# Attention of a hybrid encoder in 56 steps of four score tiles

## The chip, the cores and the metric

The kernel runs on one core of a Trainium2 chip. The metric is the time of one execution on the device in microseconds (us); lower is better. Everything is fp32 data; large products are made in three passes of split operands, and the attention's products are plain fp32, which the chip runs as two records each.

## The reference

Two layers, sequence 1024, width 1024. Each layer: RMS norm, one projection to q, k and v of three head groups, attention in each, output norm per group, output projection with residual, then a SwiGLU FFN. This part is what the change touches:

```python
oa = neighbourhood_attention(rms_norm(q), rms_norm(k), v, rpb)       # A: 4 heads, 2-D window, bias table
ob, _ = banded_attention(q, k, v, 128, slopes[:6], 1, sink)          # B: 6 query heads on 2 key heads
for window, d in ((128, 1), (512, 4), (2048, 16)):                   # C: 6 heads, three dilations
    o, lse = banded_attention(to_sub(q), to_sub(k), to_sub(v), window // (2 * d), slopes[6:], d)
oc = sum(softmax(lse) * o)                                           # merged by the denominators
y = concat([rms_norm(oa, ga), rms_norm(ob, gb), rms_norm(oc, gc)]) @ w_out
# in each: p = exp(sc - max(sc)); o = p @ v / sum(p)
```

## The kernel before, in words

Each engine has its own program, written out by hand, and they meet at semaphores. A layer runs: turned input and value projections, 14 q/k units (`qk_unit_steps`), the attention, the output projection (`out_product`), then the FFN by sums of seven block products. Only the attention changes; its ends reach into the last q/k unit and into the first output products.

The attention is a list of 224 **tiles** per layer. A tile is one head of 128 queries against a window of keys: `n_tiles` gives 24 for each of two bodies of kind c3 (dilation 16, 128 keys wide), 24 for each of two of kind c2 (dilation 4, 192 keys) and 16 for each of the eight query blocks b0, mid (six) and b7: six tiles of group B, six of C's own branch, four of A, 192 to 384 keys wide. Tiles of the dilated bodies come in 16 groups of six (one per head).

What happens to a tile:
- `score` or `score_pair` (L2125, L2133, TensorE): queries x keys into a bank. In the dilated bodies `QS` holds each head's queries padded with zero rows to 128, and a tile is one full-array product; in the blocks two heads lie on the two row halves and are issued as a pair.
- `tmin` (L1418, VectorE): table minus score, with the minimum as running accumulator; writes `T`.
- `exponential` (L1033, ScalarE): exp over `T`.
- `unit` (L2144, TensorE): transposes of `T` in chunks of 128, one unit per tile, into bank 4 or 5; `copy_unit` brings it to `PT`, even units on VectorE, odd ones on ScalarE.
- `weigh` (L2160, TensorE): `PT` x values into bank 6 or 7, in two column halves; `store_result` (L1026, ScalarE) takes each head group to `G4` or `GB`.

`pe_body` (L2185) sets TensorE's order: a dilated body takes one tile per turn, a block two: scores two ahead, transposes of the current, value products two behind. `dve_body` (L1622) follows it tile by tile and puts the finishing of a block (`own_finish`, `late_finish`: sink, merging of branches, squares, scaling of `Y`) between the tiles, one or two small operations per tile. `Y`'s parts are turned by further units (`Y_AT`) and copied to `QK`.

Beside that, GpSimd's `stage` (L1926) gathers the dilated queries of the upper half and the keys for each group (VectorE's `stage_low` the lower half), takes a power of 16 columns (`ROOTS`, L1967), and from block to block merges the branches (`merge`) and takes powers. VectorE makes A's bias tables (`bias_table`) and the last key unit's scaling (`scale_last`). SyncE's queue does, for each of the 16 dilated groups: `store_group` (L783), `spread_roots` in four of them, `load_values` for the group four later, and four loads of bias rows (L747) in the first eight.

## Time and profile before

| | |
|---|---|
| median of 3 runs | 2537.73 us (2536.75 to 2538.58) |
| the profiled execution's own time | 2537.85 us |
| its span, first to last instruction | 2536.1 us |
| TensorE busy | 2448.9 us |
| VectorE busy | 1682.6 us |
| ScalarE busy | 1061.8 us |
| GpSimd busy | 596.7 us |

Busy times are sums of records; a TensorE record is longer than the time it holds the array, as the next one starts inside it. Where TensorE's time goes is therefore read from starts: the distance from the first record of one group to the first of the next.

### The profile page before, as it was taken

The page shows a single profiled execution, that of the slowest core. Times are in us where ns is not written, and L with a number is a line of the kernel's source. Part 1 is how long each engine was busy: PE and PEld are TensorE (multiplying, and loading weights), DVE is VectorE, ACT ScalarE, POOL GpSimd, SP SyncE. Part 2 cuts the span into 40 slices and gives each one's busy share as a digit, 9 for nine tenths or more (in the row PEclk, how much of TensorE's full clock was granted, in tenths as well). Part 3 has the DMA queues.
Part 4 walks back from the last instruction along what each step waited for, and adds up shares of the span by engine and source line. Part 5 has one row for each costly group of instructions (what it writes and reads, how often), then busy time and mean ns, then how long its engine had stood idle before and what let it go on. Part 6 is the DMA issues. An engine that isn't in the chain of part 4 may idle for free. (4 is left out here: it accounts for less than half of the span.)

```text
span 2536.1 us, 39881 instructions
## 1 busy us (share of the span) xinstructions
PE 2448.9 (97%) x14416; PEld 1967.3 (78%) x14416; DVE 1682.6 (66%) x3163; ACT 1061.8 (42%) x2080; POOL 596.7 (24%) x503
## 2 busy tenths in 40 slices
PE   7999999999899999999989999999999999999998
PEld 7887666678688888888788876665777888888887
DVE  5388668864655555689844985688556555556897
ACT  4343656645322222344343336566453222223432
POOL 1000312310554454200010003123015445442000
PEclk9999999999999999999989999999999999999999
DMA  6111520033222221632351216100322222126222
GB/s 239 52 41 42 137 66 21 21 119 104 67 83 78 89 67 52 234 118 68 104 176 51 50 33 149 54 21 21 135 88 75 75 92 84 58 67 253 92 83 96
DMA packets 233420, 225.44 MB, mean 89 GB/s; under 512 B 49668, under 2 KB 191492, under 8 KB 233224
## 3 DMA queue, kind: packets, MB, share of 16 engines
q1 hardware_dynamic: 233224, 222.92, 27.9%
q8 instruction: 112, 1.84, 0.3%
q14 instruction: 84, 0.69, 0.1%
HBM read 171.03 MB, written 51.84 MB: 88 GB/s over the span
## 5 line engine op out<-in xcount | busy, mean ns | idle before, releaser
L2310 PE MATMUL psum<-OPH_t,WH 128*128 128x512 f32 x704 | 276.3, 393 | 17.3 <-DVE WL L1716 7.5
L2310 PE MATMUL psum<-OPL_t,WH 128*128 128x512 f32 x704 | 275.4, 391 | 0.0
L2310 PE MATMUL psum<-OPH_t,WL 128*128 128x512 f32 x704 | 275.3, 391 | 0.0
L1716 DVE TENSOR_TENSOR WL<-RAW,WH 128x512 fp32r<-128x512 f32 x132 | 161.5, 1224 | 161.3 <-ACT WH L1175 161.3
L2343 PE MATMUL psum<-ABH 128*128 128x512 f32 x616 | 240.1, 390 | 1.1 <-DVE X L1802 1.1
L2344 PE MATMUL psum<-ABL,ABH 128*128 128x512 f32 x616 | 239.7, 389 | 0.0
L2345 PE MATMUL psum<-ABH,ABL 128*128 128x512 f32 x616 | 239.7, 389 | 0.0
L1038 ACT ACTIVATE T<-T,G 128x192 f32<-128x192 f32 (+3 forms) x352 | 166.0, 472 | 124.8 <-DVE G L1441 121.0
L2008 POOL TENSOR_TENSOR WS<-RAW 128x512 f32<-128x512 f32 x88 | 157.5, 1789 | 211.4 <-PE psum L2040 169.5
L2310 PE MATMUL psum<-OPH_b,WH 128*128 128x512 f32 x528 | 205.6, 389 | 0.0
L2310 PE MATMUL psum<-OPH_b,WL 128*128 128x512 f32 x528 | 205.4, 389 | 0.0
L2310 PE MATMUL psum<-OPL_b,WH 128*128 128x512 f32 x528 | 205.4, 389 | 0.0
L1716 DVE TENSOR_TENSOR WL<-WS,WH 128x512 fp32r<-128x512 f32 x176 | 144.6, 821 | 83.0 <-ACT WH L1175 82.7
L2157 PE MATMUL psum<-ident,T 128*128 128x128 f32 x920 | 177.9, 286 | 16.5 <-ACT T L1038 10.7
L2038 PE MATMUL psum<-HH,UH 128*128 128x512 f32 x448 | 175.4, 392 | 5.9 <-DVE QK L1381 4.6
L2157 PEld LDWEIGHTS psum<-ident,T 128*128 128x128 f32 x920 | 105.6, 141 | 93.6 <-ACT T L1038 59.1
L2039 PE MATMUL psum<-HL,UH 128*128 128x512 f32 x448 | 175.1, 391 | 0.0
L2040 PE MATMUL psum<-HH,UL 128*128 128x512 f32 x448 | 174.9, 390 | 0.0
L1378 DVE RECIPROCAL RM<-RM 128x512 f32<-128x512 f32 x52 | 174.0, 3346 | 0.0
L2310 PEld LDWEIGHTS psum<-OPH_t,WH 128*128 128x128 f32 x704 | 133.0, 189 | 50.2 <-DVE OPL_t L1722 8.1
L1597 DVE COPY PT<-psum 128x256 f32<-128x256 f32 (+2 forms) x224 | 96.3, 430 | 104.7 <-PE psum L2157 103.9
L2310 PEld LDWEIGHTS psum<-OPH_t,WL 128*128 128x128 f32 x704 | 133.0, 189 | 27.9
(230 smaller groups left out, 5387.5 us busy)
## 6 DMA issues: line engine op xcount, KB each, us to landing
RAW<-in_w_gu SPq DMA_DIRECT2D x176, 256.0 KB, 3.8
WDS<-in_w_down SPq DMA_DIRECT2D x88, 256.0 KB, 2.7
UR<-in_w_in SPq DMA_DIRECT2D x56, 256.0 KB, 3.2
g_mid<-GRES SPq DMA_DIRECT2D x28, 512.0 KB, 2.6
WDK<-in_w_down SPq DMA_DIRECT2D x44, 256.0 KB, 5.3
x_res<-X SPq DMA_DIRECT2D x2, 4096.0 KB, 13.8
PR<-in_w_out SPq DMA_DIRECT2D x32, 256.0 KB, 4.5
X<-x_res SPq DMA_DIRECT2D x2, 4096.0 KB, 13.7
```

Source lines behind the costliest of these rows:

```text
L1038: a.activation(T[:, s % 4, off:off + w], T[:, s % 4, off:off + w], ACT.Exp, scale=-1.0, bias=G[:, 6 * V1 + place_:6 * V1 + place_ + 1]).th ...
L1378: v.reciprocal(RM[:, hf, :], RM[:, hf, :]).then_inc(rec_s, 1)
L1716: v.tensor_tensor(WL[SLOT[i, j]][:, :, :], w_source(i, j), WH[SLOT[i, j]][:, :, :].bitcast(F32), ALU.subtract).then_inc(w_lo, 1)
L2008: g.tensor_tensor(WS[i][:, :, :], first, second, op).then_inc(w_sum, 1)
L2038: t.matmul(dst, sh, mh, start=start, stop=False)
L2039: t.matmul(dst, sh, ml, start=False, stop=False)
L2040: return t.matmul(dst, sl, mh, start=False, stop=stop)
L2157: last = t.transpose(dst[0:src.shape[-1], P * i:P * i + P], src, ident[:, :])
L2310: last = t.matmul(dst[:, :], w[SLOT[i, j]][:, k, :], h[o][:, k, :], start=(i in (1, 5, 6) and k == 0 and part == 0), stop=(i in (2, 3, 4) ...
L2343: t.matmul(dst, ah, bh, start=open_, stop=False, skip_group_check=True)
L2344: t.matmul(dst, ah, bl, start=False, stop=False, skip_group_check=True)
L2345: last = t.matmul(dst, al, bh, start=False, stop=shut, skip_group_check=True)
```

## The change

The attention becomes 56 steps of four tiles, in the same order of tiles. TensorE's step k: scores of tiles 4k to 4k+3 as two pairs on row halves (now also the dilated ones: `QS` holds two heads per 128 rows, and there is no padding), the value products of step k-2's tiles, then the transposes of step k-1's tiles. Transposes are packed: up to four chunks of 128, of one or several tiles, in one bank, with one copy for each pack; the second pack of a step is copied by VectorE (in a step with one pack, that one), all others and all `Y` units by ScalarE. Banks 0, 2, 6, 7, 1, 3 rotate between scores and transposes; the value products have 4 and 5. `T` has eight slots of 384.

The (192-key) tiles of c2 now always have two chunks of 128 against a value tile whose lower rows are zeroed once; their value loads are two DMAs instead of one. `stage_low` is gone: GpSimd gathers both halves. GpSimd also takes over `bias_table`, `scale_last` (the raw unit is first kept by ScalarE's `keep_raw`) and the scaling of `Y`. VectorE's finishing of a block is regrouped into `finish(k, j)`: five places in the first step of the next block, two in its second, five in its third, none in its fourth.

```diff
-        T = sb("T", [P, 4, 640], F32, "W", 0)
-        QS = sb("QS", [P, 12, P], F32, "Q")
+        T = sb("T", [P, 8, 384], F32, "W", 0)
+        QS = sb("QS", [P, 2, 3, P], F32, "Q", 2048)
...
+            TRIO = ((0, 2), (6, 7), (1, 3))
...
+            for k in range(1, GROUPS + 1):
+                rows = steps[k]
+                for n in range(4 * k - 4, 4 * k):
+                    need = len(chunks_of(*tiles[n]))
+                    if not rows or len(rows[-1]["items"]) + need > 4:
+                        pair_ = TRIO[(k + 2) % 3] if len(rows) < 2 else TRIO[k % 3]
+                        rows.append(dict(y=None, items=[], engine=None, bank=pair_[len(rows) % 2], slot=n_pt % 4))
+                        n_pt += 1
...
+                for fam, after in (("b", 6), ("a", 7), ("c", 7)):
...
+                for i, u in enumerate(pt_rows):
+                    u["engine"] = (0 if len(pt_rows) == 1 or i == 1 else 1)
...
+            HIGH_AT = {46: 0, 49: 1, 52: 2, 54: 3}
+            PIECE_AT = {first_group(b) + 1: 13 + b for b in range(3, 7)}
...
-                return bank[2 * (s % 2) if dilated(bd) else s % 4][:, 0:width(bd, s)[0]]
+                return bank[TRIO[(n // 4 + n % 4 // 2) % 3][n % 2]][:, 0:width(*tiles[n])[0]]
...
-                        sp.dma_start(VR[:, slot, :, :], v4[(gi - 8) // 2]).then_inc(vr_in[slot], 16)
+                        sp.dma_start(VR[:, slot, 0, :], v4[j0:j0 + P]).then_inc(vr_in[slot], 16)
+                        sp.dma_start(VR[0:64, slot, 1, :], v4[j0 + P:j0 + P + 64]).then_inc(vr_in[slot], 16)
...
+                def finish(k, j):
+
+                    b, r = divmod(k - first_group(0), 4)
+                    if 0 <= b < MT and r == 2:
+                        if j == 0:
+                            own_min(b)
+                        elif j == 1:
+                            own_shift(b)
+                    b -= 1
...
+                    if r == 0:
+                        if j < 4:
+                            own_sum(b, j)
+                            if j < 2:
+                                branch_min(b, j)
+                            elif j == 2:
+                                branch_shift(b)
                         else:
...
+                            own_heads(b)
...
+                    if r == 1:
+                        if j == 0:
+                            squares(1, YB, 384, b)
+                        elif j == 1:
+                            mean(1, 384)
+                    elif r == 2:
+                        if j == 0:
+                            grid_root(b)
+                        elif j == 1:
+                            grid_heads(b)
+                            branch_root(b)
+                        elif j == 2:
+                            squares(0, YA, 256, b)
+                            branch_heads(b)
+                        elif j == 3:
                             mean(0, 256)
...
+                            squares(2, YC, 384, b)
+                        else:
+                            mean(2, 384)
...
+                    for j in range(4):
+                        if k < GROUPS:
+                            tmin(4 * k + j)
...
+                        finish(k, j)
+                    for u in steps[k]:
+                        if u["engine"] == 0:
+                            copy_unit(u)
+                    finish(k, 4)
...
+                for gi in range(C_GROUPS):
+                    stage(gi)
...
+                    elif gi in (9, 10):
+                        scale_last(gi - 9)
+                    elif gi >= 12:
+                        bias_table(gi - 12)
...
+                def first_pair_free(k):
+
+                    if k:
+                        pe.wait_ge(tmin_s, 4 * k)
+
+                def second_pair_free(k):
+
+                    if k == 1:
+                        pe.wait_ge(raw_kept, 2)
+                    elif k > 1:
+                        for u in steps[k - 1][:2]:
+                            copied(pe, u)
+
+                def pe_step(k):
+
+                    if k < GROUPS:
+                        score_pair(4 * k, lambda: first_pair_free(k))
+                        score_pair(4 * k + 2, lambda: second_pair_free(k))
...
+                    if k >= 2:
+                        for n in range(4 * k - 8, 4 * k - 4):
+                            weigh(n)
+                    for i, u in enumerate(steps[k]):
+                        if i < 2:
+                            for before in steps[k - 1][2 + i:3 + i]:
+                                copied(pe, before)
+                        else:
+                            pe.wait_ge(tmin_s, min(4 * k + 2, TILES))
+                        unit(u)
```

## Rows read from the trace of the kernel before

**Rows 1.** The page, TensorE's busy share, and one GpSimd group (busy, mean ns, idle before)

```profile
PE 2448.9 (97%) x14416; PEld 1967.3 (78%) x14416; DVE 1682.6 (66%) x3163; ACT 1061.8 (42%) x2080; POOL 596.7 (24%) x503
...
L2008 POOL TENSOR_TENSOR WS<-RAW 128x512 f32<-128x512 f32 x88 | 157.5, 1789 | 211.4 <-PE psum L2040 169.5
```

**Rows 2.** Windows: us, busy us (records) of PE, PEld, DVE, ACT, POOL; clock, DMA, GB/s

```profile
1523.00:1787.20 264.20, 254.10 (x2807) 171.03 (x2807) 193.45 (x843) 169.59 (x434) 75.81 (x85) 1.00 0.25 64
261.00:357.50 96.50, 94.02 (x878) 68.85 (x878) 57.91 (x292) 62.66 (x179) 30.30 (x29) 1.00 0.51 124
357.50:525.20 167.70, 159.96 (x1935) 102.08 (x1930) 135.71 (x551) 106.84 (x256) 45.65 (x56) 1.00 0.11 30
```

**Rows 3.** Timeline of PE, a c3 tile: start us, us to the group's end, what

```profile
273.47 0.49 PE L2131 MATMUL psum<-KS,QS 128*128 128x128 f32 x2
273.80 0.27 PE L2157 MATMUL psum<-ident,T 128*128 128x128 f32 x1
274.00 0.34 PE L2180 MATMUL psum<-VR,PT 128*64 128x65 f32 x4
274.26 0.49 PE L2131 MATMUL psum<-KS,QS 128*128 128x128 f32 x2
```

**Rows 4.** The same view, a c2 tile

```profile
322.53 0.59 PE L2131 MATMUL psum<-KS,QS 128*128 128x192 f32 x2
322.96 0.38 PE L2157 MATMUL psum<-ident,T 128*128 128x128 f32 x2
323.27 0.60 PE L2180 MATMUL psum<-VR,PT 128*64 128x65 f32 x8
323.80 0.59 PE L2131 MATMUL psum<-KS,QS 128*128 128x192 f32 x2
```

**Rows 5.** The same view, the first turn of a middle block and the next block's first

```profile
437.17 0.92 PE L2141 MATMUL psum<-QK 64*128 64x384 f32 x4
438.02 0.88 PE L2157 MATMUL psum<-ident,T 128*128 128x128 f32 x6
438.82 0.92 PE L2180 MATMUL psum<-VA,PT 128*64 128x65 f32 x24
439.67 0.55 PE L2157 MATMUL psum<-ident,Y 128*128 128x128 f32 x3
...
458.77 0.59 PE L2141 MATMUL psum<-QK 64*128 64x384 f32 x2
```

**Rows 6.** Groups by shape, DVE in that block: count, busy us, mean ns, idle before

```profile
L1441 DVE CUSTOM_DVE_ANT_0 T<-TB,psum 128x384 f32<-128x384 f32 x6 | 3.3, 547 | 0.1
L1597 DVE COPY PT<-psum 128x384 f32<-128x384 f32 x5 | 2.8, 558 | 2.4 <-PE psum L2157 2.4
L1441 DVE CUSTOM_DVE_ANT_0 T<-TC,psum 128x256 f32<-128x256 f32 x6 | 2.4, 407 | 0.0
...
L1471 DVE CUSTOM_DVE_ANT_0 junk<-Y 128x384 f32<-128x384 f32 x2 | 1.1, 552 | 0.0
...
L1534 DVE TENSOR_TENSOR Y<-G,den 128x256 f32<-128x256 f32 x1 | 0.8, 793 | 0.0
```

**Rows 7.** Timeline of SyncE's queue, dilated part: start us, us of issuing, what

```profile
270.47 1.11 SPq L789 DMA_DIRECT2D g_d<-G  x2
...
306.95 1.11 SPq L789 DMA_DIRECT2D g_d<-G  x2
...
308.88 1.91 SPq L747 DMA_DIRECT2D BIAS<-in_rpb  x4
312.79 0.35 SPq L792 DMA_DIRECT2D g_d<-G  x1
```

**Rows 8.** Timeline of GpSimd, dilated part

```profile
280.27 3.10 POOL L1967 TENSOR_TENSOR ROOTS<-ROOTS,neghalf 128x16 f32<-128x16 f32 x1 [2.70 <-DMA ROOTS<-variances]
...
284.56 0.85 POOL L1946 COPY KS<-QK 128x384 f32<-128x384 f32 x1 [0.16 <-POOL QS L1943]
```

**Rows 9.** A window between the two layers, columns as in rows 2

```profile
1265.00:1285.00 20.00, 6.08 (x38) 5.66 (x37) 11.39 (x17) 9.64 (x18) 6.56 (x12) 0.66 0.23 64
```

More of the change, by code:

```diff
@@ new lines, in build_program @@
+            t0 = g0 = 0
+            for kind, i in (("c3", 0), ("c3", 1), ("c2", 0), ("c2", 1), ("b0", 0), *(("mid", b) for b in range(1, 7)),
+                            ("b7", 7)):
+                bd = dict(kind=kind, i=i, T=t0, G=g0)
+                bodies.append(bd)
+                t0, g0 = t0 + n_tiles(bd), g0 + (4 if dilated(bd) else 3)
+            tiles = [(bd, s) for bd in bodies for s in range(n_tiles(bd))]
+            TILES, GROUPS, C_GROUPS = t0, t0 // 4, 16
+            assert g0 == C_GROUPS + 3 * MT
@@ L828, in _ @@
                     out_piece(p)
-                for parity in range(2):
-                    sp.wait_ge(pt_copied[parity], UNITS // 2)
+                for engine in range(2):
+                    sp.wait_ge(pt_copied[engine], copies[engine])
                 sp.dma_start(X[:, :, :], x_res).then_inc(x_back, 16)
@@ new lines, in _ @@
+                dve.wait_ge(table_s, C_H)
+                for k in range(GROUPS + 1):
+                    dve_step(k)
+                last = MT - 1
+                dve.wait_ge(c_fac, MT)
+                dve.wait_ge(grp_s, C_GROUPS + 3 * last + 2)
+                for i in range(3):
+                    link(v.tensor_tensor(heads(GC[:, i, :], 6), heads(GC[:, i, :], 6),
+                                         fac_c[:, i, :].unsqueeze(2).broadcast_to([P, 6, V1]), ALU.mult))
+                dve.wait_ge(tail_squares, 1)
@@ L2160, in weigh, with score_pair @@
-                def weigh(bd, s):
-                    k = bd["kind"]
-                    for idx in tile_units(bd, s):
-                        pe.wait_ge(pt_copied[idx % 2], bd["half_U"] + idx // 2 + 1)
-                    if s % 6 == 0:
+                def score_pair(n, free):
+                    bd, s = tiles[n]
+                    if dilated(bd) and s % 6 == 0:
+                        pe.wait_ge(staged, 2 * (bd["G"] + s // 6 + 1))
+                    if n == 4 * first_group(0):
+                        pe.wait_ge(qk_s, 2 * QT)
+                    free()
+                    for h in range(2):
+                        t.matmul(scores(n + h), queries(bd, s + h), keys(bd, s + h), start=True,
+                                 stop=True).then_inc(scored, 1)
@@ new lines, in unit @@
+                def unit(u):
+                    if u["y"] is None:
+                        pe.wait_ge(exp_s, u["items"][-1][0] + 1)
+                        srcs = [T[:, n % 8, c:c + P] for n, c in u["items"]]
+                    else:
+                        fam, c0, n, b = u["y"]
+                        t0_, _, fi = FAM[fam]
+                        pe.wait_ge(y_s[fi], b + 1)
+                        srcs = [Y[:, (t0_ + c0 + i) * P:(t0_ + c0 + i + 1) * P] for i in range(n)]
+                    for i, src in enumerate(srcs):
+                        last = t.transpose(bank[u["bank"]][:, P * i:P * i + P], src, ident[:, :])
+                    last.then_inc(pt_made, 1)
```

832 lines of the change are left out of this document (355 added, 477 removed).

## Prediction

> **What bounds the kernel now.** I read the page's head first: TensorE is busy for 97% of the span [rows 1]. That share is no proof of a bound, so the second view is the busy time by stage [rows 2]. The attention of one layer fills 261.0 to 525.2 us, 264.2 us, and the second layer's attention (1523.0 to 1787.2) is the same to the hundredth. It has two parts: 96 dilated tiles for 96.5 us, and eight blocks of 16 tiles for 167.7 us. In both VectorE, ScalarE and GpSimd have time left (VectorE most used, 136 of 168 us) while TensorE is busy for over 95%. Everything outside the attention is untouched, so the sum is made over these 2 x 264.2 us.
>
> The third view is TensorE's timeline, read by the distance from one group's start to the next one's, because that contains what the busy time hides. One (128,1) tile [rows 3] goes 273.47 (scores), 273.80 (transpose), 274.00 (value products), 274.26: 0.33 + 0.20 + 0.26 = 0.79 us. One (256) tile [rows 4]: 0.43 + 0.31 + 0.53 = 1.27. In a middle block [rows 5]: a score pair of 2 x 384 columns 0.85, six transposes 0.80, 24 value records 0.85.
>
> From these I take four prices. Columns: 0.33 against 0.43 for two passes of 128 and of 192 columns is 0.0008 us per column and pass. Row halves: the pair in [rows 5] takes 0.85 for two tiles; two passes of 384 at 0.0008 are 0.64, so the two heads stream at once, and 0.21 is the exposed weight load and the change to the next group. A transpose: 0.11 (two in 0.31, array already in full mode), and 0.14 on top of six times that when the mode changed before. Value products: (0.85 - 0.26) / 20 records = 0.0295 each, plus 0.14. So each change of group costs 0.14 to 0.21 us whatever it carries; the kernel pays that every tile or every two.
>
> The Trainium skill, "TensorEngine Tiling (Array Packing)", Key Properties, says that changing the tiling mode drains the engine. The trace agrees (those 0.14 to 0.21 us). It also speaks against one edit: dilated scores and transposes now share the full array, and row halves put a third change into each step. By that rule alone 24 dilated steps lose some 24 x 0.14 = 3 us per layer; the step prices below contain it.
>
> **The new step on TensorE.** Order: two score pairs, four value tiles, the transposes. Dilated (128): scores 0.21 + 4 x 128 x 0.00083 = 0.63, values 16 records 0.62, four transposes 0.58: 1.84 us per four tiles, against 4 x 0.79. Dilated (256): 0.85 + 32 records 1.08 + eight transposes 1.02 = 2.95, against up to 4 x 1.27 (the zero rows of VR also spare the change for 64-row values, [rows 4]). Middle block: 5 pairs of 384 and 3 of 256 in four groups 5.3, 42 x 4 = 168 records in four groups 5.5, 42 + 8 transposes in four groups 6.1: 16.9 us against 21.6 (437.17 to 458.77) [rows 5].
>
> **The wait that the change adds.** The second score pair waits for the copies of the first two transpose groups of the step before, because it takes their banks. Behind it on TensorE are the value products and transposes of the step. A copy of 384 columns takes 0.56, and 128 columns more cost the minima 0.14 [rows 6], so 512 take 0.70 (estimate). With about 0.3 for the way there and back the copy lands 1.0 after the last transpose; the first pair covers 0.4 to 0.6. Where the step has one or two groups (dilated, first and last block) that leaves 0.45 us per step: 3.4 us per (256) step, 2.5 per (128) step. Bounds: 0.2 (copy at once) to 0.9 (the copy queued behind a finish operation). In the middle blocks two more groups follow and cover it.
>
> **Dilated part.** Here TensorE is not what ends last. SyncE's queue issues, per group of six tiles, 2 stores, 2 value loads and 4 bias loads; from 270.47 to 310.8 it never pauses, eight rounds in 40.3 us, and idles only before 312.79 [rows 7]. None of these DMAs goes; four rounds get one more value load. A group's scores wait until the slot of four groups earlier is stored. GpSimd adds the second chain: the ROOTS power waits for a DMA of SyncE's second round and ends at 283.4, and group 5 is staged behind it, two copies of about 0.85, until 285.4 [rows 8]. The first store cannot be much earlier: the new first steps carry two raw copies and wait for them; I put it 1.5 us later. So group 5 starts at 287, and the (128) steps at 2.5 us bring group 8 to 287 + 3 x 3.8 = 298.4 (before: 300.6, of which 2 us are gained). Then eight (256) groups of 1.5 steps: 8 x 5.1 = 40.8, to 339.2. GpSimd per such group: 0.85 for the queries and 1.5 times that for 576 key columns, with waits 2.3; in the last four also the bias table taken from VectorE, 896 columns in three subtractions, between 2.0 (the copy's 2.2 ns a column [rows 8]) and 3.1 (the 3.5 ns of its own subtractions [rows 1]); I take 2.6. That is 4.9 us, just under 5.1. The two last key scalings, also moved to GpSimd, are 512 columns each, at most 1.8, and fall in rounds 9 and 10, where GpSimd has 2.8 us to spare each. The part ends at 339 instead of 357.5: 18.3 us gained per layer. Bounds: 10 (GpSimd ops half as long again: 6.2 us per group in the last four, and the slot waits 1 us each) and 27 (no copy wait).
>
> **Blocks.** VectorE sets the rest. Score minima: 384 columns 0.55, 256 columns 0.41 [rows 6], with the accumulator read inside. In the third step of a block it has four minima (1.6), a copy (0.56) and now most of the finishing: the grid heads 0.79, two squares near 0.55 [rows 6], the branch heads (384 columns, as the squares), and eight operations on a few columns and their waits, an estimated 1.3. That is 5.9 us against TensorE's 4.2. The next scores wait for its minima, the second pair for its copy: 1.7 to 1.8 us are lost there per block. The other three steps have 3 to 4.6 us on VectorE against 4.0 to 4.4. So 16.9 + 1.8 = 18.7 per middle block, 18.3 in the two without a weight piece: 112 for six. The moved work: Y's scalings go to GpSimd. It is busy for 46 of 168 us [rows 2], 5.9 per 21.6, and three scalings at the copy's 0.85 make it 8.5. Y's copies and nine of thirteen transpose copies go to ScalarE, 107 of 168 us now, 13.8 per block, then some 15.2. Both are covered; if GpSimd's sum comes 1 us late, VectorE's branch root waits and the block is 1 us longer. First block 4 x 3.4 = 13.7; last block with its two closing steps and its y work 21. Together 146.7 against 167.7: 21.0 gained. Bounds: 5 and 36 (TensorE's stream with no wait).
>
> **Sum.** Per layer 18.3 + 21.0 = 39.3; twice, 78.6. Profiled execution: span 2536.1 to 2457.5, its own time 2537.85 to 2459.2. The median of the runs is 2537.73, 0.1 lower, so the forecast is 2459 us.
>
> **Rivals.**
> A, the vector side sets every step. Each step then is VectorE's work (4.5 + 4.6 + 6.0 + 2.9 = 18.0) plus the wait for the first score pair, which it can't run ahead of, some 0.6 x 4: 20.4 per block, ten gained instead of 21, and 14 in the dilated part: 24 per layer, 2490 us. For it: minima wait for scores that TensorE issues only at the step's start. Against: steps 1, 2 and 4 have slack.
> B, TensorE's stream alone is the bound. 27 + 36 = 63 per layer, 2412 us. For it: TensorE is the fullest engine in every stage. Against: the 5.9 us step and the slot waits.
> C, slower: the clock. In 1265 to 1285 us TensorE was busy for 6 us of 20 and the granted clock was 0.66 [rows 9], a mix of the two levels, 1.2 and 2.4 GHz. The new kernel leaves TensorE idle for some 5 us before group 5 and 30% idle in the (128) steps. TensorE's attention work is 188 us per layer after the change; every us of it at the lower level costs one more. It outweighs 39.3 us from 21% on; all of it at 1.2 GHz gives 2 x (188 - 39) more, 2835 us, and 30% gives 2572. Against: the clock is 1.00 in all stages now [rows 2], at 95% busy, and would see some 84%.
> The Trainium skill, "TensorE: Matmul & The Clock Gate", Part 4, says that transposes do not count as busy in the same way; that would favour C, but the transposes now stand at 1.00.
> D, it doesn't do what it says: the row halves of the dilated scores don't stream at once, 0.43 to 0.64 per pair lost; at most 10 us per layer, 2479. It lies inside the range.
>
> **How the numbers follow.** Forecast with D's variants 0.55 (between 2435 and 2482), A 0.22 (2482 to 2505), B 0.11, C 0.06, and 0.06 for a mix that ends near no change. Eight in ten: 2425, which takes half of B, to 2495, which takes most of A. A measurement of this kernel can tell 0.2%, 5 us, from no change: faster by more 0.91, within 0.03, slower 0.06.
>
> **What would show it.** TensorE's starts: a (128) value group of 16 records in 0.62, a (256) step of 3.4 us, score pairs of 192 columns at once. SyncE's eight rounds still end near 311 to 314 and b0's first scores stand near 339. A middle block of 18.7 us with TensorE's one long gap before its last step. Wrong if the clock row falls below 0.9 in the attention, if ScalarE rather than VectorE releases TensorE's gaps, or if GpSimd's sums are late.

## Result and the profile after

| | before | after |
|---|---|---|
| median of the runs, us | 2537.83 | 2505.48 (2497.97 to 2508.53, 4 runs) |
| ratio to before, 95% interval | | 0.9868 [0.9845, 0.9891] |
| profiled execution / its span, us | 2537.85 / 2536.1 | 2503.76 / 2502.0 |
| mean granted clock over the span | 0.994 | 0.972 |
| attention, first / second layer, us | 264.2 / 264.2 | 246.0 / 247.3 (forecast 224.7) |
| of it dilated part | 96.5 | 85.0 / 86.5 (forecast 78) |
| of it blocks | 167.7 | 161.1 / 160.8 (forecast 146.7) |

The change gains 32 us, 1.3%; the forecast was 79, to 2459, with a range that ended at 2495. So the sign is right and the time lies outside. Outside the attention the two profiles differ by 1 us (2007.7 and 2008.7 us, span less the two attentions); the missing 44 us of the profiled execution are 21 and 23 us in the two attentions, two thirds of them in the blocks.

The profile's line of busy times of the kernel after, which answers to [rows 1]:

```profile
PE 2378.4 (95%) x14416; PEld 1956.2 (78%) x14416; DVE 1608.4 (64%) x2861; ACT 1063.7 (43%) x2022; POOL 673.3 (27%) x575
```

The windows, columns as in [rows 2]: the dilated part, the blocks, and a stretch of the second layer:

```profile
261.00:345.40 84.40, 69.62 (x840) 51.98 (x836) 41.79 (x215) 54.91 (x143) 43.85 (x46) 0.86 0.54 130
345.40:506.40 161.00, 142.60 (x1932) 108.69 (x1932) 113.86 (x475) 114.64 (x262) 72.10 (x77) 0.94 0.11 33
...
1510.60:1551.50 40.90, 38.95 (x294) 28.24 (x293) 18.68 (x99) 19.95 (x61) 16.61 (x17) 0.50 0.58 132
```

TensorE's busy share says little (95% against 97%). The number behind POOL's does: the clock, 1.00 in every stage of [rows 2], is 0.86 and 0.94. In the second layer there is a stretch of 41 us at 0.50, which is the lower level, 1.2 GHz, all through.

In the rows below, a bracket behind a row gives the engine's idle time just before it and what ended it. TensorE's timeline, one (128) step and one (256) step at full clock, against [rows 3] and [rows 4]:

```profile
273.19 0.49 PE L2135 MATMUL psum<-KS,QS 64*128 64x128 f32 x4
274.13 0.49 PE L2135 MATMUL psum<-KS,QS 64*128 64x128 f32 x4 [0.45 <-DVE PT L1605]
274.56 0.69 PE L2174 MATMUL psum<-VR,PT 128*64 128x65 f32 x16
275.18 0.66 PE L2148 MATMUL psum<-ident,T 128*128 128x128 f32 x4
...
316.75 0.59 PE L2135 MATMUL psum<-KS,QS 64*128 64x192 f32 x4
317.69 0.60 PE L2135 MATMUL psum<-KS,QS 64*128 64x192 f32 x4 [0.35 <-DVE PT L1605]
318.22 1.15 PE L2174 MATMUL psum<-VR,PT 128*64 128x65 f32 x32
319.30 1.09 PE L2148 MATMUL psum<-ident,T 128*128 128x128 f32 x8
```

The work is as priced: 16 value records in 0.62, the step 2.5 long, the added wait for VectorE's copy 0.35 to 0.45. The (256) step is 3.58 instead of 3.4.

A (128) step lasts 2.48 at the full clock and 3.69 at the lower level. Step lengths from one first score pair to the next, first layer, steps 0 to 11: 2.38, 4.23, 3.69, 2.48, 2.58, 2.48, 2.48, 9.53, 3.69, 3.69, 3.79, 2.48; second layer: 2.38, 3.88, 3.69, 3.69, 3.79, 3.69, 3.69, 4.92, 3.69, 3.69, 3.79, 3.69. The 9.53 is group 5, in the middle of step 7. SyncE's queue around it, against [rows 7]:

```profile
273.68 1.11 SPq L791 DMA_DIRECT2D g_d<-G  x2
...
279.64 1.13 SPq L791 DMA_DIRECT2D g_d<-G  x2
280.81 0.58 SPq L775 DMA_DIRECT2D ROOTS<-variances  x1
```

GpSimd's timeline, against [rows 8]:

```profile
282.79 2.92 POOL L1962 TENSOR_TENSOR ROOTS<-ROOTS,neghalf 128x16 f32<-128x16 f32 x1 [7.31 <-DMA ROOTS<-variances]
...
286.53 0.82 POOL L1911 COPY KS<-QK 128x384 f32<-128x384 f32 x1
```

And TensorE's first scores of group 5:

```profile
287.41 0.80 PE L2135 MATMUL psum<-KS,QS 64*128 64x128 f32 x4 [6.20 <-POOL KS L1911]
```

Group 5 starts at 287.4, forecast 287, though the first store went out 3.2 us later than before (273.68 against 270.47) and not 1.5. What the forecast left out is behind it: the clock is at the lower level from 285.1 to 302.2, and group 8 starts at 303.9 instead of 298.4.

In the blocks the steps of four tiles of the third block (first layer) are 4.03, 4.29, 6.02 and 6.35. TensorE's timeline in its third step and the first scores of the fourth, against [rows 5]:

```profile
386.82 1.13 PE L2135 MATMUL psum<-QK 64*128 64x256 f32 x8
...
392.84 0.92 PE L2135 MATMUL psum<-QK 64*128 64x384 f32 x4 [1.76 <-DVE G L1434]
```

The names used for a block's finishing, all of it on VectorE unless said: the grid heads scale A's four heads by the reciprocal of their sums; the own minimum and own shift are B's, from the sink; the branch root is the reciprocal of C's merged sums, and the branch heads scale by it. GpSimd weighs C's three branches (L1973) and adds them up (the two branch sums, L1987). VectorE's timeline, against [rows 6] (the grid heads, then the branch root):

```profile
388.58 0.42 DVE L1541 TENSOR_TENSOR Y<-G,den 128x256 f32<-128x256 f32 x1
391.01 0.19 DVE L1549 RECIPROCAL den<-G 128x6 f32<-128x6 f32 x1 [2.01 <-POOL G L1987]
```

GpSimd's (the branch weighings, the power and the scaling of Y's own part, the two branch sums):

```profile
384.30 2.55 POOL L1973 TENSOR_TENSOR G<-G,fac_c 128x390 f32<-128x390 f32 x3 [6.81 <-ACT fac_c L1059]
386.81 0.56 POOL L1935 TENSOR_TENSOR grstd<-gvare,neghalf 128x1 f32<-128x1 f32 x1
387.47 1.25 POOL L1942 TENSOR_SCALAR Y<-Y,grstd 128x384 f32<-128x384 f32 x1
388.69 2.28 POOL L1987 TENSOR_TENSOR G<-G 128x390 f32<-128x390 f32 x2
```

TensorE's idle stretch of 1.76 us is the one forecast (1.7 to 1.8), and VectorE's minima release it, as forecast. But VectorE was not at work: it stood 2.01 us before the branch root for GpSimd's two branch sums, which stood behind the scaling of Y's own part. Two minima, and so TensorE, wait behind that reciprocal:

```profile
391.11 0.38 DVE L1434 CUSTOM_DVE_ANT_0 T<-TC,psum 128x256 f32<-128x256 f32 x1
...
392.36 0.41 DVE L1434 CUSTOM_DVE_ANT_0 T<-TC,psum 128x256 f32<-128x256 f32 x1
```

The fourth step then pays once more. Two windows of another block, the idle stretch and the step behind it:

```profile
450.50:454.70 4.20, 2.22 (x29) 1.68 (x24) 4.17 (x20) 1.92 (x5) 1.96 (x2) 1.00 0.01 4
454.70:461.10 6.40, 6.21 (x63) 4.32 (x63) 4.14 (x15) 4.99 (x11) 3.69 (x4) 0.73 0.20 63
```

And a group of that step, 1.36 to the next group's start (at 458.75), where 24 value records at full clock take 0.75:

```profile
457.39 1.57 PE L2174 MATMUL psum<-VB,PT 128*64 128x65 f32 x24
```

### The profile page after: what moved, and what is told of

The parts are those of the page before. It is cut to its first block and busy times, and to the rows that moved or that the text cites. A ratio compares the mean times of both kernels' runs of the same rounds, so it can differ in the third digit from the quotient of the medians.

```text
span 2502.0 us, 39097 instructions
## 1 busy us (share of the span) xinstructions
PE 2378.4 (95%) x14416; PEld 1956.2 (78%) x14416; DVE 1608.4 (64%) x2861; ACT 1063.7 (43%) x2022; POOL 673.3 (27%) x575
## 5 line engine op out<-in xcount | busy, mean ns | idle before, releaser
L1049 ACT ACTIVATE T<-T,G 128x192 f32<-128x192 f32 (+3 forms) x352 | 157.5, 468 | 104.4 <-DVE G L1434 103.1
L1697 DVE TENSOR_TENSOR WL<-WS,WH 128x512 fp32r<-128x512 f32 x176 | 144.7, 822 | 82.8 <-ACT WH L1194 82.8
L2318 PEld LDWEIGHTS psum<-OPL_t,WH 128*128 128x128 f32 x704 | 132.8, 189 | 27.3
L1910 POOL COPY QS<-QK 128x384 f32<-128x384 f32 x32 | 28.8, 900 | 463.4 <-DVE QK L1390 256.3
L2039 PE MATMUL psum<-PH,HH 128*128 128x512 f32 (+1 forms) x384 | 143.7, 374 | 0.0
## 6 DMA issues: line engine op xcount, KB each, us to landing
x_res<-X SPq DMA_DIRECT2D x2, 4096.0 KB, 13.7
```

Source lines behind the costliest of these rows:

```text
L1049: a.activation(T[:, n % 8, off:off + w], T[:, n % 8, off:off + w], ACT.Exp, scale=-1.0, bias=G[:, 6 * V1 + place_:6 * V1 + place_ + 1]).th ...
L1697: v.tensor_tensor(WL[SLOT[i, j]][:, :, :], w_source(i, j), WH[SLOT[i, j]][:, :, :].bitcast(F32), ALU.subtract).then_inc(w_lo, 1)
L2039: t.matmul(dst, sh, mh, start=start, stop=False)
L2318: last = t.matmul(dst[:, :], w[SLOT[i, j]][:, k, :], h[o][:, k, :], start=(i in (1, 5, 6) and k == 0 and part == 0), stop=(i in (2, 3, 4) ...
```

## Experiments

Four lengths are read from each trace: the dilated part and the blocks' part in either layer (from the first scores to the first block's, and from there to the first output product). "Step" is a step of four tiles; a block has four, and its first four tiles make the first.

| kernel | median us | ratio to before [95%] | dilated | blocks |
|---|---|---|---|---|
| the change | 2505.5 | 0.9868 [0.9845, 0.9891] | 85.0 / 86.5 | 161.1 / 160.8 |
| e1_filler | 2492.0 | 0.9798 [0.9768, 0.9827] | 87.6 / 89.2 | 154.8 / 154.8 |
| e2_power | 2496.8 | 0.9831 [0.9815, 0.9848] | 81.8 / 83.0 | 161.8 / 160.8 |
| e3_power_bias | 2512.3 | 0.9901 [0.9885, 0.9918] | 87.0 / 91.2 | 159.2 / 159.7 |
| e4_finish | 2507.8 | 0.9877 [0.9860, 0.9893] | 85.9 / 85.2 | 160.8 / 162.3 |
| e5_order | 2498.2 | 0.9837 [0.9816, 0.9859] | 84.2 / 84.8 | 158.6 / 159.3 |
| e6_late | 2501.4 | 0.9846 [0.9828, 0.9865] | 85.5 / 85.7 | 158.6 / 156.0 |
| e7_merge_finish | 2493.7 | 0.9823 [0.9805, 0.9841] | 80.5 / 83.9 | 157.3 / 155.7 |
| e8_blocks | 2478.2 | 0.9766 [0.9749, 0.9782] | 86.9 / 81.3 | 148.2 / 148.5 |
| e9_merge | 2480.1 | 0.9780 [0.9761, 0.9799] | 81.3 / 81.3 | 148.0 / 147.9 |
| e10_power_order | 2471.1 | 0.9739 [0.9723, 0.9756] | 80.1 / 83.1 | 147.7 / 147.7 |
| e11_bias | 2469.3 | 0.9730 [0.9713, 0.9746] | 80.2 / 75.9 | 147.7 / 147.7 |
| e12_filler | 2456.2 | 0.9675 [0.9659, 0.9691] | 74.1 / 76.2 | 147.9 / 147.8 |
| e13_filler_only | 2497.7 | 0.9828 [0.9810, 0.9845] | 85.1 / 80.6 | 160.9 / 159.6 |
| e14_merge_late | 2473.7 | 0.9745 [0.9729, 0.9762] | 85.8 / 82.2 | 144.3 / 144.7 |
| e15_all | 2450.8 | 0.9647 [0.9627, 0.9667] | 74.1 / 75.6 | 144.8 / 144.2 |
| e16_bias_later | 2444.7 | 0.9624 [0.9608, 0.9640] | 70.7 / 70.7 | 144.7 / 144.9 |

The dilated part's code is the same in the change, e4, e6, e7, e8, e9 and e14, and its length goes from 80.5 to 86.9 per layer: it depends on where the clock falls. Outside the attention, where all these kernels have the same code, the profiled executions take from 2007 to 2015 us. So differences of a few us between medians, or between dilated parts, are not clear of this spread, and the blocks' column is what the blocks' edits are judged by. The four lengths are those of one execution each.

**Is it the clock? e1_filler.** Identity matmuls where TensorE stands idle:

```diff
+for _ in range(count):
+    t.matmul(target[:, 390:512], ident[:, :], ident[:, 0:122], start=True, stop=True)
...
+filler(k, {1: 7, 2: 0, 7: 20}.get(k, 1 if 1 < k < 12 else 0))
...
+if k > 24 and k % 4 == 2:
+    filler(k + 1, 7)
```

> The changed kernel with fillers on TensorE: float32 matmuls of the identity (128 rows, 122 columns) into the unused columns of the result bank, placed only where it stands idle (7 before the second score pair of step 1, 20 in step 7 before group 5, one per other (128) step, 7 at the end of each block's third step). They add no wait for another engine and change nothing else. Theory 'clock': the steps after the gaps are long because the granted clock falls to the 1.2 GHz level there. Then the clock row reads 1.00 in the attention, a block's fourth step falls from 6.0-6.4 to 4.8 us and the second layer's (128) steps from 3.7 to 2.5: 7 x 1.4 in the blocks and 3 to 5 in the dilated part of each layer, some 26 us in all, near 2480. Rival 'waits': those steps are long because they wait for copies and minima, and the clock only goes with it; then the fillers give under 5 us or cost time, 2500 to 2515.

In the blocks it is the clock: 1.00 over both block parts, the fourth step 4.5 to 4.8 in every middle block, the part 6.2 us shorter though the first block, where there was no idle stretch, pays 1.05 for its fillers (15.57 against 14.52). So the clock costs the blocks some 7 us per layer, where 7 x 1.4 = 9.8 had been expected; the third steps kept their 6.0 and 6.5. In the dilated part the 20 fillers were no cure: group 5 still waited behind them, the clock fell at 288.5, and the steps with a filler came to 4.29: the part is 2.6 and 2.8 us longer instead of 3 to 5 shorter. Both put the time 12 us above the expectation.

**GpSimd's power. e2_power.**

```diff
-                    elif gi == 4:
+                    elif gi == 5:
                         pool.wait_ge(root_s, SPREAD_IN)
```

> The ROOTS power on GpSimd is issued behind the staging of group 5 instead of ahead of it; nothing else moves. Theory 'GpSimd chain': group 5's scores wait 6.2 us for staging that stands behind this power, which waits for a DMA. Then that wait is under 3 us, and the dilated part falls from 85-86 us to 80-81 per layer: 8 to 10 us in all, near 2496. Rival 'SyncE queue': the stores and loads of SyncE, five us per group, come next in line at the same moment; the wait only moves from group 5 to the minima or the value products of groups 5 and 6, the part keeps 85 us, and the time stays within 2 us of the changed kernel's 2505.

As the first theory had it, step 7 goes from 9.53 to 2.57 and the time is 2497. But the rival has its share: steps 13 and 14 are now 5.4 and 6.0 (3.1 and 3.6 in the change), VectorE's minima there waiting up to 3.4 us for the store of G4, so that of 7.0 us 4.7 come back. The part is 3.2 and 3.5 us shorter where 4 to 5 had been expected, and 81.8 and 83.0 lie inside the spread of the unchanged code: the wait that is gone is shown, its price in time is not clear of the clock.

**SyncE's bias loads. e3_power_bias.**

```diff
-                    if gi < 2 * A_H:
-                        load_bias(gi // 2, gi % 2)
+                    if 2 <= gi < 2 + 2 * A_H:
+                        load_bias((gi - 2) // 2, gi % 2)
...
-                    pool.wait_ge(rpb_in, 128 * (h + 1))
+                    pool.wait_ge(rpb_in, 128 * A_H)
```

> As the kernel with the moved ROOTS power, and the bias loads of SyncE issued in rounds 2 to 9 instead of 0 to 7, so that rounds 0 and 1 have two or four DMAs less to issue. If SyncE's queue is what ends last in the dilated part, store 1 goes out 2 to 3 us earlier and the part ends 3 to 6 us earlier than with the power alone: 76 to 78 us per layer, the value forecast (78), near 2486. If GpSimd's chain was all of it, this adds under 1 us per layer; if the later rounds, now with eight DMAs, become the bound, the part is as long as with the power alone or longer.

A miss, and an instructive one: the (128) steps of the first layer now run at 2.5 from step 3 on, but GpSimd's bias tables wait 11.1 us for the last loads with group 13's staging queued behind them; one step of 12.3 us (9.0 in the second layer) eats all. The wait is the edit's own: its second line lets the first table wait for all four heads' loads, issued until 322.4, where before it waited for its own head's, issued here by 291.2. So this run says little of SyncE's queue. The queue behind a moved wait had not been counted.

**VectorE's third step. e4_finish.** Own minimum, own shift, branch squares and mean go to the fourth step (and with them ScalarE's own factors, to the fourth tile's place):

```diff
-                    if 0 <= b < MT and r == 2:
+                    if 0 <= b < MT and r == 3:
...
-                            squares(2, YC, 384, b)
-                        else:
-                            mean(2, 384)
+                    elif r == 3:
+                        if j == 0:
+                            squares(2, YC, 384, b)
+                        elif j == 1:
+                            mean(2, 384)
```

> In every block three pieces of VectorE's small work go from the third step to the fourth: own minimum, own shift, and the branch squares with their mean. Same operations, same count. Theory 'third step': the third step lasts 5.8 to 6.5 us only because VectorE has all this between its minima, TensorE idles 1.8 us before the fourth, and the clock falls in it. Then the third step falls to 4.4-4.8, the fourth stays at 4.8 with the granted clock at 1.00, a middle block goes from 20.8 to 18.7, and the kernel gains 7 x 2 per layer: near 2478. Rival 'VectorE's sum': what leaves the third step is missing in the fourth, which then lasts as much longer; gain under 5 us, 2500 to 2505.

Both expectations miss in their reason. The third step lost 0.17 in the third block and 0.23 in the next three, although about 1 us of VectorE's work had left it. VectorE's timeline says what took its place:

```profile
412.04 0.19 DVE L1549 RECIPROCAL den<-G 128x6 f32<-128x6 f32 x1 [0.91 <-POOL G L1989]
```

So VectorE's list alone does not set the third step, as the forecast of the blocks had it. This run made me read the same reciprocal in the changed kernel (2.01, above).

**Copies before the second pair. e5_order.**

```diff
                         score_pair(4 * k, lambda: first_pair_free(k))
+                        if 12 <= k < 28:
+                            for n in range(4 * k - 8, 4 * k - 4):
+                                weigh(n)
                         score_pair(4 * k + 2, lambda: second_pair_free(k))
```

> In steps 12 to 27 (the (256) steps and the first block) TensorE's value products are issued between the two score pairs instead of behind both, so that the second pair's wait for the copies of the step before has 1.1 us of work ahead of it. Theory 'copy wait': a (256) step lasts 3.58 us because TensorE idles 0.35 there and changes group once more; it should fall to 3.1-3.25, 15 such steps give 5 to 7 us per layer, near 2494. Rival 'queues': GpSimd and SyncE set the pace of the (256) groups (5.4 us per group now, 1.5 steps), then the step means stay at 3.5 and the time within 2 us of the changed kernel's.

The (256) steps go from 3.58 to 3.53, 3.16, 3.53: mean 3.41, 0.17 each and 0.6 in the first block, some 2.6 us per layer. Half of what was expected (the 7 us between the medians hold other differences of the clock too): the wait moves to the copies behind, for two steps of three.

**Weight pieces. e6_late.** The high parts go to ScalarE's third steps, the low parts to VectorE's steps one to three later:

```diff
-            HIGH_AT = {46: 0, 49: 1, 52: 2, 54: 3}
-            PIECE_AT = {first_group(b) + 1: 13 + b for b in range(3, 7)}
+            HIGH_AT = {46: 0, 50: 1, 53: 2, 54: 3}
+            LOW_AT = {49: 0, 53: 1, 54: 2, 55: 3}
+            PIECE_AT = {first_group(b) + 2: 13 + b for b in range(3, 7)}
+            PIECE_LOW_AT = {first_group(b) + 5: 13 + b for b in range(3, 7)}
```

> The early weight pieces and the four early rows of the output operand: ScalarE's high part moves to steps where it has time (a block's third step), VectorE's low part to a later step in which its source has long been there. So VectorE no longer stands 1.6 us before a block's third step and 1.1 to 1.8 us before three others. Theory 'third step has two chains' (VectorE's own list, and GpSimd's sums that the branch root waits for): alone it gives little, the third step goes from 6.46 only to the 6.0 of the blocks without a piece, because GpSimd's sums end at the same moment; the steps 49-50 (7.9 us) lose 1.5: 4 to 5 us per layer, near 2496. Rival 'VectorE's list alone': the third step falls by the whole wait, 1.6, and with it the clock loss: 9 or more per layer, under 2487.

VectorE's wait for ScalarE, ahead of the third step of the change's sixth block, was this one:

```profile
449.88 0.69 DVE L355 TENSOR_TENSOR PL<-PR,PH 128x512 fp32r<-128x512 f32 x1 [1.62 <-ACT PH L351]
```

The steps are as the two-chain theory has them: the third goes from 6.46 to 6.02 and 6.35 only, the last middle block from 23.3 to 20.8. The blocks lose 2.4 and 4.9 us, and the time is 5 us over the expectation.

**GpSimd's order with the finish move. e7_merge_finish.**

```diff
-                    mean_powers(1, b)
-                    scale_y("b", b)
                     for i in (1, 2):
                         pool.wait_ge(merge_s, 5 * b + 2 + i)
                         g.tensor_tensor(GC[:, 0, 0:6 * V1], ...
+                    mean_powers(1, b)
+                    scale_y("b", b)
```

> The kernel that moves three pieces of VectorE's work from the third step to the fourth, and on GpSimd the two branch sums issued ahead of the scaling of Y's own part (1.8 us) instead of behind it. The finish move alone gave nothing: VectorE then waited 0.91 us for GpSimd's sums. Theory 'two chains': with both the third step falls below 5.3 in blocks without a piece and to about 5.6 in those with one, near 2490 to 2497. Rival: some third thing (ScalarE's copies) holds the step at 6: no change against 2508.

The third step falls to 4.8 and 4.96 in blocks without a piece, 5.9 with one (5.6 expected); the time is inside the interval given.

**The three edits together. e8_blocks.** e4's, e6's and e7's.

> All three: the weight pieces and output rows where they wait for nobody, GpSimd's sums first, VectorE's three pieces in the fourth step. Theory 'two chains and the clock': the third step comes to TensorE's own 4.4-4.6, no idle stretch over 0.5 us is left in a middle block, the clock row of the blocks is 1.00, the fourth step 4.8-5.0; a middle block 17.6 to 18.0 and the blocks' part 138 to 142 per layer against 161: near 2462. Rival: the gains don't add, the load only moves; above 2480.

The blocks fall to 148.2 and 148.5, 12.6 us less, where e6 and e7 alone gave 3.7 and 4.5: together they also bring the clock to 1.00 and 0.99. That is not the 138 to 142 expected: the fourth step is 5.39 in all middle blocks, not 4.8, as TensorE waits 0.8 us in it for the scaling of Y's branch part. e14, without the finish move, has 4.83 there; so the move was a mistake that this kernel still carries.

**The order alone. e9_merge.** The same diff as e7's last, on the changed kernel.

> The changed kernel with GpSimd's two branch sums ahead of the scaling of Y's own part, alone; it closes the square with the finish move (alone 2508) and the two together (2494). Theory 'two chains side by side': a block's third step goes from 6.02 to between 5.5 and 6.0 only, because VectorE's own list takes about as long; the fourth still finds the clock low in most blocks; within 5 us of the changed kernel: 2500 to 2508. Rival 'GpSimd's sums alone set the step and the finish move adds nothing': the third step falls to 5.0 by this edit alone, near 2494.

The largest miss of the series, and the answer: the rival is right. Two statements moved by a few lines give 25 us in the median. In the profiled execution, the shortest of the four (2468.3), the blocks are 26.1 us shorter in both layers together, and the dilated parts, whose code is unchanged, 8.9. GpSimd's timeline in the third block, to be read beside that of the change:

```profile
377.46 2.56 POOL L1973 TENSOR_TENSOR G<-G,fac_c 128x390 f32<-128x390 f32 x3 [6.81 <-ACT fac_c L1059]
380.10 2.12 POOL L1985 TENSOR_TENSOR G<-G 128x390 f32<-128x390 f32 x2
```

VectorE's branch root:

```profile
382.57 0.18 DVE L1549 RECIPROCAL den<-G 128x6 f32<-128x6 f32 x1
```

TensorE's fourth step, its first scores and 24 value records:

```profile
384.69 0.92 PE L2135 MATMUL psum<-QK 64*128 64x384 f32 x4
...
386.64 0.92 PE L2174 MATMUL psum<-VB,PT 128*64 128x65 f32 x24
```

And the window of the blocks' part:

```profile
339.60:487.50 147.90, 135.85 (x1933) 102.03 (x1933) 112.77 (x475) 113.58 (x262) 73.25 (x77) 1.00 0.12 36
```

The sums end at 382.2, before VectorE asks for them; the third step is 4.70, the stretch before the fourth is gone, the clock is 1.00 over the whole part and the fourth step 4.83 (the 24 value records take 0.75, to 387.39). I had taken VectorE's list for as long as its chain; it isn't: with all its work in place the step is 4.70.

With e4 and e7 this closes a square of two edits, and the blocks (mean of the layers) read: change 161.0, finish move alone 161.6, both 156.5, order alone 147.9.

**Dilated part on mended blocks. e10_power_order, e11_bias, e12_filler.** Each adds one edit to the one before: the power and the order; the bias loads in rounds 2 to 9 with two tables behind the last staging; seven fillers in step 1.

> The kernel with the mended blocks (2478) and, in the dilated part, the ROOTS power behind group 5's staging and the value products between the score pairs in steps 12 to 27. If the terms add: the power gives 3.3 per layer, the order 2.5 to 3, so 11 to 13 together, near 2466. If SyncE's queue of stores is what ends last there, the order's gain is eaten in the waits before steps 13 to 15 and only the power's remains: 2471 or more.

> As the kernel with the mended blocks, power and order, with SyncE's bias loads in rounds 2 to 9, and what waited for them made later: the bias tables behind groups 14, 15 and the last staging, and the last key scaling behind groups 11 and 12. The earlier try lost 9 to 12 us in one step because the tables waited in GpSimd's queue ahead of group 13's staging; that wait is then gone. If SyncE's queue is the bound of the dilated part once GpSimd's wait is gone, the waits before steps 13 to 15 (3.3 to 5 us) shrink: 3 to 4 us per layer less, near 2460, and the dilated part near 76, close to the 78 forecast. If the clock alone is what is left, no change.

> As the kernel before it, with seven filler matmuls (about 1.5 us) on TensorE while it waits for the raw copies in step 1, and nothing more. The only idle stretch before the long low stretch of the clock (second layer: 41 us from step 1 on, steps of 3.7 instead of 2.5) is that one of 1.96 us. If it brings the fall, the (128) steps are 2.5 from step 2 on in both layers: up to 12 x 1.2 in the second, 2 to 3 x 1.2 in the first, 8 to 16 us less. If the 20 to 30% idle time spread over the (128) steps brings it anyway, no change or a fall a few steps later.

The first gives 7 of the 12 us, as its second sentence has it (steps 13 and 14 at 5.2 and 6.2). The bias loads give 1.8 in the median where some 10 were expected. Their effect shows between two layers with the same low stretches of the clock (6.8 and 3.4 us), e10's first and e11's second: 80.1 against 75.9; elsewhere the clock covers it. With the filler the median is 13 us lower, within what was expected, and the (128) steps are 2.4 to 2.6 from step 2 on in both layers. That is worth 5.5 and 2.0 us there; of the 11.1 us between the two profiled executions 5.5 lie in the attention and the rest outside it, in the same code.

**The filler alone. e13_filler_only.**

> The changed kernel with seven filler matmuls (1.5 us) in the 1.96 us stretch of step 1 in which TensorE waits for the raw copies; nothing else. If that stretch brings the long low stretches of the clock: the (128) steps are 2.5 us from step 2 to group 5, in both layers; but group 5 then waits for GpSimd as long as before or longer, so that only part of it stays: 3 to 9 us in all, 2496 to 2502, and the blocks keep their low clock (the fourth steps stay at 6.0 to 6.4). If the clock does not hang on this stretch: 2505 and steps of 3.7.

TensorE's step 1 in it (the identity matmuls are the filler):

```profile
262.68 1.82 PE L2211 MATMUL psum<-ident 128*128 128x122 f32 x14
264.73 0.49 PE L2135 MATMUL psum<-KS,QS 64*128 64x128 f32 x4 [0.22 <-ACT QK L1031]
```

As expected: steps 2 to 6 at 2.4 to 2.6 in both layers, then group 5's step at 9.98 and 9.91. In the first layer nothing is left of it (85.1): the clock falls in that wait, for 23.9 us from 281.0 on. In the second it stays up behind the wait, and 5.9 us are left. So the faster steps before group 5 only make the wait for GpSimd longer; to gain from them both must be mended.

**Sums and pieces, nothing else. e14_merge_late.** 

> The changed kernel with GpSimd's two branch sums first, and the weight pieces and output rows where they wait for nobody; VectorE's list stays as it is. The sums alone left 4.70 us for the third step of a block without a piece and 6.04 with one. Theory: with both all middle blocks have 4.7 to 5.0 (GpSimd's sums and the pieces were the whole excess over VectorE's list), and fourth steps of 4.83; 4 x 1.2 us per layer less than with the sums alone, 2468 to 2472, the blocks' part 141 to 144 us. Rival: as in the kernel with the finish move, third steps stay at 5.4 where ScalarE makes a piece; above 2474.

The steps come as stated: 4.70, or 5.06 from the fifth block on (5.63 in the last middle block), and 4.83. The part is 144.3 and 144.7, 3.4 less than with the sums alone. The part is 0.3 and 0.7 over the expectation. The median is 1.7 over; the profiled execution, 2469.0, is inside.

**All of it. e15_all, e16_bias_later.**

> Sums first, pieces moved, ROOTS power behind group 5, value products between the score pairs in steps 12 to 27, bias loads in rounds 2 to 9 with their tables later, filler in step 1; VectorE's list untouched. Against the kernel with the finish move (2456): third and fourth step 9.5 us together instead of 10.4 to 10.8, six blocks per layer: 10 to 14 us less, 2442 to 2446, if the terms add.

> As the kernel with all of it, the bias loads in rounds 5 to 12 instead of 2 to 9, and all four bias tables behind the last staging. VectorE's minima of groups 8 and 9 wait up to 3 us for the stores of SyncE's rounds 4 and 5. If SyncE's queue is the bound of the dilated part there, these waits (2.1 + 0.5 + 0.7 us before steps 13 to 17) go, the part falls from 74 to about 71, and 4 to 6 us in all are gained. If not, the time is the same, or longer where the tables come too late for the first block's fourth step.

e15 is 5 to 9 us over its expectation: against e12 the blocks give 3.4 per layer where I had counted 5 to 7. e16 is as expected. A wait of VectorE's minima in e15:

```profile
298.97 0.35 DVE L1436 CUSTOM_DVE_ANT_0 T<-TC,psum 128x192 f32<-128x192 f32 x1 [3.01 <-DMA g_d<-G]
```

The windows of e16, dilated part and blocks:

```profile
260.80:331.40 70.60, 63.09 (x856) 47.55 (x856) 41.23 (x215) 53.37 (x144) 34.80 (x34) 1.00 0.63 148
331.50:476.10 144.60, 136.89 (x1931) 104.02 (x1932) 116.05 (x475) 113.48 (x262) 81.60 (x89) 0.98 0.14 40
```

With four DMAs less in SyncE's rounds 2 to 4 the wait for the store of G4 is gone, no step of the dilated part waits for a queue any more, and both layers agree to 0.2 us. It is the fastest kernel here: 2444.7 us, 3.8% below before and 2.4% below the change, from the same 56 steps with only issue places and seven fillers altered.

## Why the prediction was wrong

Two steps failed. The clock was priced at nothing, and that is the largest term of what is missing. And "VectorE sets the rest" is wrong: GpSimd's queue sets a block's third step. The second did not move the number, since the wrong cause had the right length.

**The sum for the blocks (146.7; measured 161).** Right: the prices of TensorE's groups, the first two steps of a block (4.0 and 4.3), the idle stretch before the fourth step and its length. Wrong is the step "VectorE sets the rest". Its 5.9 us for the third step matched the measured 6.0 by chance. VectorE's own list is at most the 4.70 of e9: the grid heads, priced 0.79 from [rows 6], take 0.42, and the copy (0.56) and one of the squares (0.55), counted in the 5.9, stand behind the last minimum, for which the next scores wait (392.36, 392.77, 393.24 in the change). What ended last was GpSimd's chain: three weighings 2.55, a power 0.56, a scaling 1.25, two sums 2.28, from ScalarE's factors on. I had priced GpSimd as a sum (8.5 of 18.7 us, "both are covered") where its order decided; the text named the case ("if GpSimd's sum comes 1 us late") and gave it 1 us. Mending the order alone gives 13.0 us per layer (e9).

**The clock (priced at nothing).** Rival C was made for a fall over a large part of the work, and the sum has no term for a fall over a part of it. The text's own test, a clock row below 0.9, came true in the dilated part (0.86). Inside the 13.0 of e9 the clock is some 7 (e1); in the dilated part it turns 2.48 into 3.69 for 4 to 9 of the twelve steps. A forecast that says "1.7 us of idle time before the fourth step" should have asked what the step behind it runs at: of the twelve fourth steps of middle blocks in both layers eight came at 6.0 or more and four at 4.83, the length at full clock.

**Pieces (not priced).** A piece is 512 columns of a weight of the output projection, of which ScalarE makes the high part and VectorE the low one. The low part on VectorE stands 1.62 us for ScalarE's high part ahead of the third step: 3.4 us per layer (e9 to e14). The sum had no term.

The 14.3 missing in the blocks come to: the clock some 7 (e1); the pieces 3.4; the fourth step, at full clock 4.83 where the sum's 16.9 leaves 4.4, in six blocks 2.6; the first block 0.8 (14.5 against 13.7). That is 13.8. The part of e9's 13.0 that is not the clock, some 6, is not among them: the sum had that wait, put down to VectorE.

**The dilated part (78; measured 85.0 and 86.5).** Right: 2.5 per (128) step, group 5 at 287, 41.5 us from group 8 to the first block (forecast 40.8). The (256) step was 0.18 under, but the first two were shorter than forecast (2.58 and 3.11): 0.7 us in all. Wrong: from group 5 on the steps were priced at full clock, and group 8 came 5.5 us late. Of the limits, the power costs a wait of 7.0 us before group 5, of which 4.7 come back behind it (e2), SyncE's queue is the next (e15 to e16: 3.4 and 4.9 us), and the clock in step 1 is worth 5.5 us of (128) steps in the first layer and 2.0 in the second, which had it up sooner (e11 to e12).

**The working.** Rival D's 0.43 to 0.64 us are those of a step of two pairs, not of a pair. The 0.79 of the grid heads held a wait, and [rows 6] could not show it; the last section has the rows.

**The rivals.** A (the vector side sets every step, 2490) is nearest in time and wrong in its reason: three of four steps ran at TensorE's pace. C was right in kind. The Trainium skill's rule that transposes don't count as busy in the same way ("TensorE: Matmul & The Clock Gate", Part 4) is not borne out as a cause by itself: e9 has every transpose of the change and a clock of 1.00 over the blocks. D is refuted, the row halves stream at once: 64 columns more per head make a pair 0.10 longer (0.43 and 0.53 in the rows above), which is two passes at 0.0008 and not four.

**What stays open.** Why the clock falls behind some idle stretches of 1.8 us and not behind others, and so why the same dilated code takes 80.5 to 86.9 us. No run was made for it. The lengths read from one profiled execution of each kernel can't say how often each case comes.

## What to carry to other kernels

Price a busy engine by its order, not by its share: follow the one value that the waiting engine needs back through the queue that makes it, and count what stands ahead of it there. Where a change makes TensorE wait once in every round, add what the work behind costs at half the clock, from a row, and look for filler work or, better, for what makes it wait. A step that fits its forecast may still have another cause: before an edit that relies on it, read who releases whom in the trace of after.

## What the runs showed of the chip

**The granted clock** fell to 0.50 behind idle stretches of 1.8 to 2 us (step 1; the third step of the blocks), and stayed there for up to 41 us, although TensorE was busy for 38.95 of 40.90 us in them. 1.8 us of identity matmuls, whose results nobody reads, kept it at 1.00 in step 1 and up to the wait before group 5 (e13).

**VectorE and GpSimd in each other's way.** The own minimum, 6 columns of two SBUF operands, takes 0.16, and 0.64 while GpSimd adds (two blocks of the change, and GpSimd's sums beside the second):

```profile
387.94 0.16 DVE L1483 TENSOR_TENSOR nmin<-GB,GAINS 128x6 f32<-128x6 f32 x1
...
450.83 0.64 DVE L1483 TENSOR_TENSOR nmin<-GB,GAINS 128x6 f32<-128x6 f32 x1
...
450.12 2.42 POOL L1987 TENSOR_TENSOR G<-G 128x390 f32<-128x390 f32 x2
```

So do a piece's subtraction (0.69 and 1.49) and the grid heads (0.42 and 1.26), while the score minima, with one operand in PSUM, stay at 0.41. The Trainium skill, "SBUF — State Buffer", "SBUF: two separate sides", has VectorE's second SBUF operand and GpSimd behind one exclusive lock. For GpSimd's tensor_tensor the trace agrees (0.16 against 0.64). For its tensor_scalar it does not: the 0.16 at 387.94 lies inside the scaling of Y that runs from 387.47 for 1.25 us, as do five more own minima of the change, none longer than 0.16. There the measurement decides.

The 0.79 that the prediction took for the grid heads from [rows 6] held such a wait. In the trace of before all 14 of them start while GpSimd weighs a branch, end some 0.3 us behind the end of that operation and take 0.67 to 1.00; in the change the ten with no GpSimd operation beside them take 0.41 to 0.43. The one of [rows 6]:

```profile
447.95 0.79 DVE L1534 TENSOR_TENSOR Y<-G,den 128x256 f32<-128x256 f32 x1
...
446.83 2.62 POOL L1980 TENSOR_TENSOR G<-G,fac_c 128x390 f32<-128x390 f32 x3
```
